# First FFN: input pairs 5 to 17 as seven block products, and the pieces of the modulation vector moved out of them

## What is computed

```python
cond = silu(c)
mod = cond @ w_ada[l] + b_ada[l]
sh1, sc1, gt1, sh2, sc2, gt2, sh3, sc3, gt3 = split(mod, 9)
u = modulate(rms_norm(h, g_ffn1[l]), sh1, sc1)
h = h + 0.5 * gt1 * swiglu(u, w_ffn1_in[l], w_ffn1_out[l])
u = modulate(rms_norm(h, g_mix[l]), sh2, sc2)
h = h + gt2 * hybrid_mixer(u, w_in[l], ...)      # 8 stick-breaking heads, 4 delta-net heads
u = modulate(rms_norm(h, g_ffn2[l]), sh3, sc3)
h = h + 0.5 * gt3 * swiglu(u, w_ffn2_in[l], w_ffn2_out[l])

def swiglu(u, w_in, w_out):                      # w_in: 1024 x 5632, w_out: 2816 x 1024
    a, b = split(u @ w_in, 2)
    return (silu(a) * b) @ w_out
```

## Time and profile before

| | us |
|---|---|
| median of 3 runs | 1198.93 |
| lowest, highest | 1198.72, 1199.66 |
| profiled execution | 1196.75 |
| its span in the trace | 1195.0 |

### The profile page before, as it was taken

The page is one execution under the profiler, slowest core; times in us unless marked ns, Lnnn a source line. Parts: engine busy times, 40 slices in busy tenths (PEclk is TensorE's granted clock), DMA queues, the critical chain, the costliest instruction groups (busy, mean ns, idle before and its releaser), DMA issues.

```text
span 1195.0 us, 20070 instructions
## 1 busy us (share of the span) xinstructions
PE 1179.7 (99%) x7503; PEld 993.5 (83%) x7503; DVE 826.4 (69%) x1219; ACT 556.9 (47%) x843; POOL 60.3 (5%) x98
## 2 busy tenths in 40 slices
PE   7999999999999999999999999999999999999998
PEld 5788888888888887777787878888889999998887
DVE  5666676665665694777587566666789999988552
ACT  5423232322222585676773536544446666653331
POOL 1000000000111000000402110003000000000000
PEclk9999999999999999999999999999999999999999
DMA  9777666776564233221233132653233333342440
GB/s 326 230 205 210 199 176 187 210 211 192 160 167 115 56 104 89 71 54 53 71 89 91 53 96 66 211 153 95 71 106 106 106 105 103 102 132 78 115 115 27
DMA packets 235053, 152.51 MB, mean 128 GB/s; under 512 B 8021, under 2 KB 216046, under 8 KB 234990
## 3 DMA queue, kind: packets, MB, share of 16 engines
q1 hardware_dynamic: 230890, 149.62, 43.4%
q10 hardware_dynamic: 4100, 2.02, 0.6%
HBM read 145.31 MB, written 6.29 MB: 127 GB/s over the span
## 4 chain that ended last, share of the span: by engine, by line
PE 93%; DVE 3%; ACT 2%; DMA 1%; issue 1%; SPq 0%; ACTq 0%; DVEq 0%
PE tail L2224 8%; PE tail L2228 7%; PE tail L2233 7%; PE region L2224 7%; PE region L2233 7%; PE region L2228 7%; PE tail L2214 5%; PE region L2315 5%; PE region L2319 5%; PE region L2312 5%; PE tail L2216 5%; PE tail L2215 5%; PE region L2214 2%; PE region L2216 2%; PE region L2215 2%; PE tail L2312 1%
## 5 line engine op out<-in xcount | busy, mean ns | idle before, releaser
L785 ACT ACTIVATE w_hi<-raw 128x1024 fp32r<-128x1024 f32 (+1 forms) x160 | 179.1, 1119 | 359.7 <-PE region L2233 161.3
L1366 DVE TENSOR_TENSOR w_lo<-raw,w_hi 128x1024 fp32r<-128x1024 f32 (+1 forms) x158 | 205.9, 1303 | 92.5 <-ACT w_hi L785 92.4
L2214 PE MATMUL tail<-u_hi,w_hi 128*128 128x512 f32 x264 | 107.6, 408 | 0.9 <-DVE w_lo L1366 0.9
L2216 PE MATMUL tail<-u_hi,w_lo 128*128 128x512 f32 x264 | 103.2, 391 | 0.0
L2215 PE MATMUL tail<-u_lo,w_hi 128*128 128x512 f32 x264 | 103.0, 390 | 0.0
L2224 PE MATMUL region<-u_hi,w_hi 128*128 128x512 f32 x368 | 91.1, 390 | 0.1
L2233 PE MATMUL region<-u_hi,w_lo 128*128 128x512 f32 x368 | 90.9, 389 | 0.0
L2228 PE MATMUL region<-u_lo,w_hi 128*128 128x512 f32 x368 | 90.9, 389 | 0.0
L2224 PEld LDWEIGHTS region<-u_hi,w_hi 128*128 128x128 f32 x368 | 68.9, 188 | 15.2 <-issue 0.6
L2228 PEld LDWEIGHTS region<-u_lo,w_hi 128*128 128x128 f32 x368 | 69.1, 188 | 14.4
L2233 PEld LDWEIGHTS region<-u_hi,w_lo 128*128 128x128 f32 x368 | 69.1, 188 | 14.3
(11 more groups left out here) (492 smaller groups left out, 2332.7 us busy)
## 6 DMA issues: line engine op xcount, KB each, us to landing
raw<-in_w_ffn_in SPq DMA_DIRECT2D x168, 256.0 KB, 3.5
ada_raw<-in_w_ada SPq DMA_DIRECT2D x56, 512.0 KB, 5.2
raw<-in_w_in SPq DMA_DIRECT2D x90, 256.0 KB, 3.3
raw<-in_w_ffn_out SPq DMA_DIRECT2D x32, 384.0 KB, 5.3
raw<-in_w_ffn_out SPq DMA_DIRECT2D x32, 320.0 KB, 4.5
ada_early<-in_w_ada SPq DMA_DIRECT2D x8, 1024.0 KB, 10.7
gates<-kept_gates SPq DMA_DIRECT2D x16, 256.0 KB, 2.9
raw<-in_w_out SPq DMA_DIRECT2D x16, 256.0 KB, 3.2
```

Of the source, the lines that this page charges most:

```text
L785: act.activation(w_hi[:, slot % 2, 0:k, :], raw[:, slot, 0:k, :], ACT.Copy).then_inc(hi_ready, 1)
L1366: dve.tensor_tensor(w_lo[:, slot % 2, 0:k, :], raw[:, slot, 0:k, :], w_hi[:, slot % 2, 0:k, :].bitcast(f32), ALU.subtract).then_inc(lo_rea ...
L2214: pe.matmul(bank(b), wh, xh, start=start and n == 0, stop=False)
L2216: ins = pe.matmul(bank(b), wl, xh, start=False, stop=stop and n == k - 1)
```

## The change

- Pairs 5 to 17 of the first FFN get the seven-product form. The functions get an argument f (0 for the first FFN, 1 for the second), and the first FFN its own tiles for the token sums, which lie over parts of `g_hi`, `g_lo` and of slots 2 and 3 of `ada_raw`. Its weight sums lie in unused columns 8 to 10 of `raw`.
- The loop of the first FFN's input now runs over i = 3 to 7, with pairs 0 to 5 and 16 to 21 written out.
- The token sums for this are made in pairs 0 to 3: `full_tokens` (four instructions of 128x1024) behind `g_lo` of pair 0, the four `token_sums` around the product of pair 1, their high parts on ScalarE in pairs 1 and 2, their low parts on VectorE in pairs 2 and 3.
- Pieces of the modulation: 16 in the input stage (table `PIECES`: none in pairs 5 to 16), 28 in the output stage (four for each of seven chunks), and 12 in attention, one in each unit m = 2 to 13, loaded row by row. `ada_rows` follows where four are complete. Rounds 2 and 3 change places with 4 and 5, so that the scale row is there in time.
- `ada_totals(0)` goes from the end of the input stage to behind the first unit of the output stage, and VectorE waits for it before the second. `ada_totals(1)` comes in the last lap of the output stage, `ada_totals(2)` and `gate_columns(1)` before the mixer's output product.

```diff
-MOD_ROUNDS = (0, FF // P // 2 - 1, (MODS * KD - LATE) // 4)
+ROUND_AT = (0, 1, 4, 5, 2, 3) + tuple(range(6, ROUNDS))
+MOD_ROUNDS = (0, 4, 6, ROUNDS)
+PIECES = {1: (0,), 2: (1, 2), 3: (3, 4), 4: (5,), 17: (6, 7), 18: (8, 9), 19: (10, 11), 20: (12, 13), 21: (14, 15)}
+OUT_PIECE = 4 * MOD_ROUNDS[1]
+BY_ROWS = OUT_PIECE + 4 * (D // P - 1)
...
-MIX_0, MIX_LAST = 5, KF - 1
+MIX_0, MIX_LAST = (5, 5), (17, KF - 1)
...
-                ada_raw = sb("ada_raw", [P, 2, ROWS, 4 * P], stack=t)
+                ada_raw = sb("ada_raw", [P, 4, ROWS, 4 * P], stack=t)
...
+            def load_rows(m):
+
+                for n in range(ROWS):
+                    q = BY_ROWS + m - PAIR_0
+                    sp.wait_ge(ada_step, 2 * q + n - 1)
+                    sp.dma_start(ada_raw[:, 3, n], piece_source(q, q % 4, n, n + 1)[:, 0, :]).then_inc(ada_in[2 + n], 16)
...
+                if PAIR_0 <= n - DN_IN < PAIR_0 + 12:
+                    load_rows(n - DN_IN)
...
-                for i in laps(act, KF // 2, 3 if f else 1):
+                for i in laps(act, KF // 2, 3, 1 if f else KF // 2 - LAST_MIX_STEP):
...
-                        if f and is_static(i) and i == 1:
-                            tokens_hi(((0, 2), (1, 3))[jj])
+                        if is_static(i) and j in (2 - (not f), 3 - (not f)):
+                            tokens_hi(f, ((0, 2), (1, 3))[j - 2 + (not f)])
...
+            def row_pieces(m):
+
+                q = BY_ROWS + m - PAIR_0
                 for n in range(ROWS):
...
+                    dve.wait_ge(ada_in[2 + n], out_pieces_in(2, D // P - 2) + 16 * (m - PAIR_0 + 1))
+                    ada_row(q, 3, q % 4, n)
+                if q % 4 == 3:
+                    ada_rows(q // 4)
...
+                if f == 0 and j == 0 and place == 2:
+                    full_tokens(0)
+                for n in ((0,), (1,), (2, 3))[place]:
+                    if j == 1 + f:
+                        token_sums(f, n)
...
+                        if f == 0 and not last:
+                            out_pieces(o, (0, 1))
...
+                            out_pieces(o, (2, 3))
+                            ada_rows(MOD_ROUNDS[1] + o)
...
             ffn_in(0, F1_IN)
+            ada_rows(MOD_ROUNDS[1] - 1)
             ada_mods(0)
...
                 split_lo(DN_IN + m + 2, 0, 0)
                 convolve(m)
+                if PAIR_0 <= m < PAIR_0 + 12:
+                    row_pieces(m)
...
                 convolve(pair_unit(p, 0))
+                row_pieces(pair_unit(p, 0))
                 mixed(pair_unit(p, 1))
...
             ffn_in(0, F1_IN)
-            ada_totals(0)
...
-            ffn_out(0, 0, F1_OUT, lambda i, oo: None)
+            def after_half(i, oo):
+
+                if is_static(i) and oo == 0:
+                    ada_totals(1 if i else 0)
```

More of the change, by code:

```diff
@@ L91, in mod_batch @@
 def mod_batch(row):
-    return 1 if (row * KD + KD - LATE) // 4 <= MOD_ROUNDS[1] else 2
+    own = [ROUND_AT.index((row * KD - LATE) // 4 + n) for n in range(2)]
+    return next(n for n in range(1, 4) if max(own) < MOD_ROUNDS[n])
 def first_tile(k):
@@ L138, in mixes, with nth, pairs_mixed @@
 def mixes(f, i, jj):
[L140 to L148, removed]
+    return not is_static(i) or MIX_0[f] <= 2 * i + jj <= MIX_LAST[f]
+def nth(f, i, jj, steps, name, before):
+    return 2 * len(steps) * i + (len(steps) * (jj - MIX_0[f]) + before + steps.index(name) + 1)
+def pairs_mixed(f):
+    return MIX_LAST[f] - MIX_0[f]
@@ L150, in counted @@
+def counted(f, i, jj, name, first, steps, last, former):
     j = 2 * i + jj if is_static(i) else None
-    if j == MIX_0 and name in first:
-        return first.index(name) + 1
+    before = len(first) + former
+    if j == MIX_0[f] and name in first:
+        return former + first.index(name) + 1
     if name + "+" in steps:
-        return nth(i, jj - 1, steps, name + "+", len(first))
-    return nth(i, jj, steps, name, len(first)) if j != MIX_LAST else \
-        nth(i, jj, steps, steps[0], len(first)) + last.index(name)
@@ L884, in mixed_pair @@
                 x, z = mix_banks(jj)[0], mix_banks(jj)[2]
                 ahead = (2 * jj + 2) % RAW
-                next_a = (F2_IN + ahead) % RAW
-                act.wait_ge(mix_ps, product_done(i, jj, "p1"))
-                act.wait_ge(raw_in[next_a], raw_mix(2 * jj + 2, i))
-                quad_hi(w_hi[:, mix_a, top, :], raw[:, next_a, top, :])
+                next_a = ((F1_IN, F2_IN)[f] + ahead) % RAW
+                act.wait_ge(mix_ps, product_done(f, i, jj, "p1"))
+                act.wait_ge(raw_in[next_a], raw_mix(f, 2 * jj + 2, i))
@@ L890, in mixed_pair @@
+                quad_hi(f, w_hi[:, mix_a[f], top, :], raw[:, next_a, top, :])
                 if not first:
-                    g_high(j - 1)
-                act.wait_ge(glu_ready, KF + j)
-                snapshot(work[:, 0, halves[0]], x)
+                    g_high(f, j - 1)
+                act.wait_ge(glu_ready, KF * f + j)
+                snapshot(f, work[:, 0, halves[0]], x)
                 if not last:
                     act.wait_ge(unit_done, n + 1)
-                    act.activation(w_hi[:, mix_a, low_half, :], raw[:, next_a, low_half, :], ACT.Copy).then_inc(hi_ready, 1)
@@ L897, in mixed_pair @@
[L897 to L903 removed]
+                    act.activation(w_hi[:, mix_a[f], low_half, :], raw[:, next_a, low_half, :], ACT.Copy).then_inc(hi_ready, 1)
@@ L904, in mixed_pair @@
+                act.wait_ge(mix_ps, product_done(f, i, jj, "p5"))
+                act.wait_ge(g_lo_ready, KF * f + j)
+                snapshot(f, work[:, 1, halves[1]], z)
+                act.wait_ge(sums_done, summed(f, i, jj, "s3"))
+                quad_hi(f, w_hi[:, mix_b[f], top, :], s3[f][jj % 2])
+                act.wait_ge(mix_ps, product_done(f, i, jj, "p6"))
+                snapshot(f, work[:, 0, halves[1]], x)
                 if last:
-                    act.activation(w_hi[:, mix_a, out_rest, :], raw[:, next_a, out_rest, :], ACT.Copy).then_inc(hi_ready, 1)
+                    act.activation(w_hi[:, mix_a[f], rest_of_a[f], :], raw[:, next_a, rest_of_a[f], :], ACT.Copy).then_inc(hi_ready, 1)
@@ L1683, in ffn_in @@
                                           ALU.subtract).then_inc(g_lo_ready, 1)
-                        if turn:
-                            for n in (2, 3):
-                                token_sums(n) if jj == 0 else tokens_lo(n)
-                        if f == 0:
-                            if not (is_static(j) and j == 0):
-                                for k in range(2):
-                                    ada_late(2 * j - 2 + k, k, 2 * (1 - jj) + k, j)
+                        tokens(f, j, 2)
+                        if f == 0 and is_static(j):
+                            in_pieces(j)
             def ffn_out(s, f, phase):
```

483 lines of the change are left out of this document (265 added, 218 removed).

## The result

The changed kernel takes 1207.49 us where the kernel before takes 1198.93. That is the median of five executions, one of them disturbed (2565.43 us), which the ratio leaves out; the other four took 1205.5 to 1207.5 us, with 1206.7 in the middle. The ratio is 1.0064, 95% interval 1.0047 to 1.0082: slower by 0.64%, 7.7 us. The prediction was 1204.0, range 1198.0 to 1208.5. The profiled execution has a span of 1204.1 us for 1195.0, 9.1 more.

A forecast was written before the change was run, and what follows sets the result against it. TensorE, carrying 93% of the chain of waits, was taken to bound the kernel. The terms -10.7 + 2.1 + 2.2 + 0.9 + 0.3 + 10.3 = +5.1 us, put on the median 1198.93, gave 1204.0, range 1198.0 to 1208.5.

The forecast's parts named there:

- The gain: First FFN's input: 13 pairs go from 10.88 to 10.06 us each with seven products, -10.7 us.
- Rival 4: First FFN: seven-product pairs don't keep the pace, strided columns of `raw` costing VectorE more; +4 us, 1208; chance 0.11.
- Pair 3: Start of the first FFN: pair 3's weights ready on ScalarE at 63.9, wanted at 62.00; +2.1 us.
- Pair 5 and pair 6: Entry into the seven-product form: VectorE late with split weights, +2.2 us at pair 5 and +0.9 at pair 6.
- Output stage: Entry into the first FFN's output stage: `ada_totals(0)` waits for round 3, +0.3 us with a restart.
- Attention: Head pairs: pieces ahead of `ysb_lo` delay the next scores by 1.9, 3.3, 3.5 and 1.6 us; sum +10.3.
- so the loss comes back each time and nothing in TensorE's fixed order can fill it: Attention: closed loop of scores, ScalarE, keep and `ysb_lo`, repeating the loss in each head pair; sum +10.3 us.
- the 0.48 that I took off: Head pair 3: TensorE's 0.48 us idle in waits on ScalarE was to absorb part of 2.1, leaving 1.6.
- the forecast case: Whole kernel: slower by 5.1 us, 1204.0 us; chance 0.66.

The follow-up runs named there:

- e4: The changed kernel with the seven products from pair 7 in place of pair 5; 1205.31 us, ratio 1.0045 against the kernel before.
- e3: The kernel before with 8, 6 and 5 additional idle sums on VectorE ahead of `ysb_lo` in head pairs 0, 1 and 2; 1213.77 us, ratio 1.0128.
- e1: The changed kernel with the 12 pieces by rows moved from units 2 to 13 (attention) to units 14 to 25; 1208.47 us, ratio 1.0076.
- e7: The kernel of e6 with the seven products from pair 7; 1198.59 us, ratio 0.9998 against the kernel before.
- e2: The changed kernel with all three pieces of a head pair behind `ysb_lo` in VectorE's queue; 1200.49 us, ratio 1.0015.
- e9: The changed kernel with only its 12 pieces moved, to units 4, 7, 10, 13, 14, 18, 20, 22, 23, 25, 28, 30; 1196.88 us, ratio 0.9989.
- e5: The changed kernel with the 12 pieces at units 4, 7, 10, 13, 14, 22, 23, 27, 28, 30, 31, 32; 1202.34 us, ratio 1.0027.
- e6: The kernel of e5 with `full_tokens`, the token sums and their high and low parts one pair later; 1204.51 us, ratio 1.0052.

## Why the prediction was right, and where a size was off

By its own steps, in the profiled executions:

- **The gain.** 13 pairs x 0.82 = 10.7 us predicted; pairs 7 to 17 take 10.05 us each, the pace of the second FFN. Rival 4 has fallen: the strided columns cost VectorE nothing that shows.
- **Pair 3.** +2.1 predicted; its weights are ready at 62.69 + 1.04 = 63.73, 63.9 predicted, and it starts at 63.88 for 62.00: +1.88. Pair 5 starts at 85.75, 1.99 us later than two plain pairs behind 62.00.
- **Pair 5 and pair 6.** +2.2 and +0.9 predicted; 12.30 and 11.01 us for 10.06: +2.24 and +0.95. e4 shows that VectorE's lateness is the cause.
- **Output stage.** +0.3 predicted. TensorE's first matmul there is at 263.45 for 269.27 (-5.82), its statistics behind the stage at 385.78 for 390.33 (-4.55): +1.27. The wait for the totals is 0.45, the two small products that left the input stage are some 0.36 more, and the rest, 0.5 us, I put down to restarts that I had not counted; it wasn't taken apart. 0.3 us of it is given back ahead of attention.
- **Attention.** +10.3 predicted, +14.74 measured (104.20 to 118.94). The gaps were right: 1.65, 3.07, 3.32 and 1.89 us. The step that was mis-sized is "so the loss comes back each time and nothing in TensorE's fixed order can fill it": I took the loss for the gap alone, with TensorE's own work behind it as long as before. From the scores' start to the next weight unit it was 3.14 us in every head pair; it is 5.92 in head pair 2 (527.38 to 533.30) and 4.78 in head pair 3 (559.65 to 564.43). That is 2.78 + 1.64 = 4.4 us, all of the miss: 6.20 - 2.78 = 3.4 for 3.5, and 3.68 - 1.64 = 2.0 for 2.1 before the 0.48 that I took off. e3 shows that the gap alone does it.
- **Behind attention** 1.1 us come back (9.91 late at 589.32, 8.82 at the merge), 0.48 of it the two small waits in the second stretch of the earlier trace rows, which I had booked in head pair 3; only one of them (0.23) is for ScalarE, the other (0.25) for VectorE's `w_lo`.

-10.7 + 2.0 + 2.2 + 1.0 + 1.0 + 14.7 - 1.1 = +9.1: the span of 1204.1. Two terms that this leaves out cancel: 0.3 us less in the input stage, where the two small products no longer stand, and 0.3 more behind the merge (8.82 late there, 9.1 at the end). Without the clock's 4.4 us it would have been +4.7, for +5.1 predicted.

The median rose by 8.6 us and the ratio says 7.7: still the forecast case, at the upper edge of its range. That the time stayed inside it is in part luck: the top, 1208.5, was set by rival 4, which turned out to be worth nothing, and what filled the place was a term that stands in none of the rivals.

## What to carry to other kernels

Work for an engine with idle time costs nothing only if it is put where that engine is idle: count from the instruction that someone waits for back to where its queue was last empty, and the few tenths to spare there are the price list, not the share of busy time. The same 12 pieces cost attention 14.7 us with two of three ahead of `ysb_lo`, 7.9 with all behind it and nothing with one in a head pair, and in a stage with more idle time on average they cost about as much as in attention (e1). When a gap of TensorE is predicted to be over some 2 us, give it a second price: here the scores ran at half rate behind it and took 1.6 to 2.8 us more, and behind gaps of 1.8 to 1.9 us they sometimes did. And for work moved, follow its loads as well: e7's largest wait came from rows in SyncE's queue ahead of the gates.

## What the runs showed of the hardware

The granted clock falls to 1.2 GHz in or just behind short gaps in an otherwise dense stream. In the profiled executions, from pair 3 on, it fell at every gap of TensorE from 2.37 us on (2.37, 2.65, 2.80, 3.07, 3.32, 3.36, 3.68, 3.92, 4.54, 5.10 and 6.13 us) and stayed up behind all from 1.14 to 1.57 us. In between there is no clean border, and the same gap at the same place has two outcomes. Behind 1.83 to 1.85 us at pair 3 it stayed up in the executions of the changed kernel, of e1, e2, e4 and e9, and fell in that of e5. Ahead of head pair 1's scores it stayed up behind 1.65 us in the changed kernel and fell behind 1.83 in e4; ahead of the product behind attention it stayed up behind 1.89 us in the changed kernel and fell behind 1.87 in e4. And in e5, e6 and e7 it was at 0.50 from 2 to 3 us behind the gap of 1.67 or 1.68 us in the chain of small matmuls of the delta network, which is less dense around it (0.34 us busy of 2.00 from 708 to 710 us in e7). It was back at 1.00 some 3 to 6 us behind the end of a gap, and 9 us behind it in the delta network. What decides between 1.6 and 2.4 us stays open.

On VectorE, independent sums of 128x512 start some 0.60 us apart when nothing is between them (in e7 the four `ydn_lo` take 2.49 us, the last of them 0.69: 1.80 / 3). Those of e3, each of which waits for the semaphore of the one before and writes the same tile, start 0.71 us apart; which of the two makes the difference wasn't tested.
